# Last attention: query-key scores as two products of rounded parts, output copies on ScalarE, weight slabs dealt anew

## The reference

```
def stick_breaking_attention(q, k, v):
    ...
        valid = (key_pos[None, :] < q_pos[:, None]) & (key_pos[None, :] >= pad)
        zlog = jnp.einsum('bqhd,bkhd->bhqk', qi, kp) * scale
        log_beta = jax.nn.log_sigmoid(zlog)
        log_keep = jnp.where(valid, log_beta - zlog, 0.0)
        after = lax.cumsum(log_keep, axis=3, reverse=True) - log_keep
        w = jnp.where(valid, jnp.exp(log_beta + after), 0.0)
        return jnp.einsum('bhqk,bkhd->bqhd', w, vp)
```

## Time and profile before

| | us |
|---|---|
| median of 3 runs | 1615.33 (1614.38 to 1616.31) |
| the profiled execution: its own time | 1612.91 |
| its span in the trace | 1611.1 |
| busy in the span: TensorE (PE) | 1546.4 (96%) |
| VectorE (DVE) | 1024.8 (64%) |
| GpSimd (POOL) | 885.3 (55%) |
| ScalarE (ACT) | 507.3 (31%) |
| granted TensorE clock over the span | 0.992 |
| the last attention | about 850 to 1136 |

### The profile page before, as it was taken

How to read it: one execution, slowest core, us unless ns; L and a number is a source line. 1 busy time by engine, 2 the same in 40 slices (tenths; PEclk the granted TensorE clock), 3 DMA queues, 4 the chain that set the end, 5 groups by cost and what they waited for, 6 DMA issues and landing times.

```text
span 1611.1 us, 28791 instructions
## 1 busy us (share of the span) xinstructions
PE 1546.4 (96%) x10686; PEld 1352.3 (84%) x10686; DVE 1024.8 (64%) x1602; ACT 507.3 (31%) x1047; POOL 885.3 (55%) x830
## 2 busy tenths in 40 slices
PE   5999999999999999999988999998999999999998
PEld 4888877897888888999987888887998998988886
DVE  4499847469828876865767878875336666565002
ACT  4311012131137763333345555554214110111001
POOL 1455431567684408663428744344572777777981
PEclk9999999999999999999999999999999999999999
DMA  9437421323210002232111111112131333333331
GB/s 320 125 118 210 156 72 53 92 66 92 79 52 2 23 6 79 79 92 65 41 40 50 43 53 53 39 44 62 53 92 40 91 91 91 91 94 111 121 118 52
DMA packets 188971, 131.11 MB, mean 81 GB/s; under 512 B 5279, under 2 KB 171711, under 8 KB 188751
## 3 DMA queue, kind: packets, MB, share of 16 engines
q1 hardware_dynamic: 188878, 129.82, 26.5%
HBM read 127.71 MB, written 2.10 MB: 81 GB/s over the span
## 4 chain that ended last, share of the span: by engine, by line
PE 87%; DVE 7%; ACT 3%; issue 2%; DMA 1%; SPq 0%; DVEq 0%; ACTq 0%
PE ps L2316 20%; PE ps L2317 19%; PE ps L2319 19%; PE ps L3048 3%; PE ps L3047 3%; PE ps L3046 3%; PE ps L2640 2%; PE ps L2664 2%; PE ps L2961 2%; DVE sb_sum L2147 2%; PE ps L2627 1%; DMA ada_first<-in_ada_w 1%; DVE op_lo L1538 1%; PE ps L2869 1%; PE ps L2937 1%
## 5 line engine op out<-in xcount | busy, mean ns | idle before, releaser
L773 POOL TENSOR_SCALAR w_hi<-raw 128x512 fp32r<-128x512 f32 x322 | 244.4, 759 | 600.3 <-PE ps L2319 229.2
L775 POOL TENSOR_TENSOR w_lo<-raw,w_hi 128x512 fp32r<-128x512 f32 x322 | 462.2, 1435 | 26.8
L2316 PE MATMUL ps<-xn_hi,w_hi 128*128 128x264 f32 (+1 forms) x800 | 234.2, 313 | 8.5 <-ACT q_even L1285 3.3
L2316 PE MATMUL ps<-op_hi,w_hi 128*128 128x512 f32 x608 | 215.6, 355 | 1.6 <-DVE op_lo L1538 1.4
L2317 PE MATMUL ps<-xn_lo,w_hi 128*128 128x264 f32 (+1 forms) x800 | 212.7, 286 | 0.0
L2317 PE MATMUL ps<-op_lo,w_hi 128*128 128x512 f32 x608 | 204.9, 354 | 0.0
L2319 PE MATMUL ps<-op_hi,w_lo 128*128 128x512 f32 x608 | 177.9, 352 | 0.0
L2316 PEld LDWEIGHTS ps<-xn_hi,w_hi 128*128 128x128 f32 x800 | 152.1, 190 | 21.9 <-issue 13.5
L2316 PE MATMUL ps<-u_hi,w_hi 128*128 128x258 f32 (+1 forms) x528 | 162.1, 321 | 0.9 <-DVE u_lo L2208 0.4
L2319 PE MATMUL ps<-xn_hi,w_lo 128*128 128x264 f32 (+1 forms) x800 | 162.9, 285 | 0.0
L2317 PE MATMUL ps<-u_lo,w_hi 128*128 128x258 f32 (+1 forms) x528 | 162.0, 320 | 0.0
(11 more groups left out here) (458 smaller groups left out, 3211.2 us busy)
## 6 DMA issues: line engine op xcount, KB each, us to landing
raw<-in_w_in SPq DMA_DIRECT2D x45, 512.0 KB, 3.6
raw<-in_w_up SPq DMA_DIRECT2D x44, 512.0 KB, 3.7
ada_ring<-in_ada_w SPq DMA_DIRECT2D x14, 1024.0 KB, 5.3
raw<-in_w_down SPq DMA_DIRECT2D x22, 512.0 KB, 3.2
raw<-in_w_in_ab SPq DMA_DIRECT2D x20, 512.0 KB, 5.5
raw<-in_w_in_c SPq DMA_DIRECT2D x20, 512.0 KB, 3.7
ada_first<-in_ada_w SPq DMA_DIRECT2D x4, 2048.0 KB, 16.4
raw<-in_w_out SPq DMA_DIRECT2D x16, 512.0 KB, 3.8
```

The source lines that it names most:

```text
L773: steps(nc.gpsimd.tensor_scalar(hi, r, 1.0, 0.0, ALU.mult, ALU.add))
L775: nc.gpsimd.tensor_tensor(lo, r, hi.bitcast(F32), ALU.subtract)\
L2316: mm(o[:, 512 * b:512 * b + n], w_h[:, k, :], hi[:, k0 + k, c0:c0 + n], start=a, stop=False)
```

## The change

- **Scores.** Queries and keys are split into a rounded part and the rest, as the weights are. For each head of a pair, `qs` holds the rounded queries in the head's own 64 rows and their rest in the other 64 rows; `k1` holds the rounded keys in both halves; `k2` holds the rest of the keys in the head's own rows and zeros in the others. A score is then two fp32r products over 128 rows, q by `k1` and q by `k2`, in place of one fp32 product. Only unit 0 keeps plain fp32, with two products as well.
- **Copies of a slab.** `take` now copies the slab once to a staging tile `staged_sb`. `take_hi` makes the rounded parts of the two heads (two copies of 64 rows). `other_rows`, for keys only, copies the staged keys rounded into the other half (two more). GpSimd makes the rests in `low_parts`: two operations of 64 rows for queries and two for keys. `take` of keys waits for the rests of the queries, `take` of values for those of the keys (`sb_lo`); scores of a pair wait for `sb_hi` and `sb_lo`.
- **Output copies** go from VectorE to ScalarE, behind the copies of transposed weights of the step.
- **VectorE's step** begins with the scan; the operand for the norm comes last. The scan writes over its input (`sb_sum` is `sb_relu`), so that `sb_start` waits for an older transpose.
- **Tables.** `SB_CHUNKS` and `SB_TAKE` deal the chunks to other steps: queries are finished in step 3 (before: 4), keys in step 6 (7), values in step 0 (9 or 0). GpSimd's sum of squares moves one slab on.

```diff
-        SB_CHUNKS = {0: 4, 2: 3, 3: 3, 4: 2, 5: 3, 6: 3, 7: 2, 8: 4, 9: 4,
-                     11: 3, 12: 3, 13: 2, 14: 3, 15: 3, 16: 2, 17: 4}
-
-        SB_TAKE = {0: (0, 2, -1), 4: (1, 0, 0), 7: (1, 1, 1), 9: (1, 2, 2), 13: (0, 0, 3), 16: (0, 1, 4)}
+        SB_CHUNKS = {0: 3, 2: 4, 3: 4, 4: 3, 5: 2, 6: 3, 7: 2, 8: 3, 9: 3,
+                     11: 4, 12: 4, 13: 3, 14: 2, 15: 3, 16: 2, 17: 3}
+
+        SB_TAKE = {0: (0, 2, -1), 3: (1, 0, 0), 6: (1, 1, 1), 9: (1, 2, 2), 12: (0, 0, 3), 15: (0, 1, 4)}
...
+            def low_parts(pair, kind, splits):
+
+                m = pair % 2
+                pool.wait_ge(s["split"], splits)
+                pool.wait_ge(s["sb_hi"], 3 * pair + kind + 1)
+                for half in range(2):
+                    h = head_rows(half)
+                    if kind == 0:
+                        staged(nc.gpsimd.tensor_tensor(qs[m][head_rows(1 - half), half, :], staged_sb[h, :],
+                                                       qs[m][h, half, :].bitcast(F32), ALU.subtract))
+                    else:
+                        staged(nc.gpsimd.tensor_tensor(k2[m][half][h, :], staged_sb[h, :],
+                                                       k1[m][h, half, :].bitcast(F32), ALU.subtract))
+                pool.sem_inc(s["sb_lo"], 1)
...
             for g in range(-2, 24):
+                if g % 3 == 0:
+                    low_parts(g // 3, 1, g0 + 3 + g)
...
                 slab((g0 + 3 + g) // 2, (g0 + 3 + g) % 2, True)
+                if g % 3 == 2 and (g + 1) // 3 < SB_PAIRS:
+                    low_parts((g + 1) // 3, 0, g0 + 4 + g)
...
-                if g >= 4 and g % 3 == 1:
+                if g >= 5 and g % 3 == 2:
                     ysb_square(g // 3 - 1)
...
+            def take(m, kind, n, i=0):
+
+                act.wait_ge(s["slab_done"], g0 + n + 6 * i)
+                if kind:
+
+                    act.wait_ge(s["sb_lo"], (n - 1) // 3 * 2 + kind + 4 * i)
+                nc.scalar.activation(two(staged_sb[:, :]), seg2(gemm_ps[0]), ACT.Copy,
+                                     scale=1.0 if kind else ATT_SCALE).then_inc(s["sb_evac"], 1)
+
+            def take_hi(m, kind, n, i=0):
+
+                act.wait_ge(s["sb_evac"], n + 6 * i)
+                for half in range(2):
+                    h = head_rows(half)
+                    ins = nc.scalar.copy((k1 if kind else qs)[m][h, half, :], staged_sb[h, :])
+                ins.then_inc(s["sb_hi"], 1)
+
+            def other_rows(m):
+
+                for half in range(2):
+                    ins = nc.scalar.copy(k1[m][head_rows(1 - half), half, :], staged_sb[head_rows(half), :])
+                ins.then_inc(s["sb_hi"], 1)
...
+                    for w in sb_out_now(u - SB_SKEW) if sb_live(i, u - SB_SKEW) else ():
...
+                        act.wait_ge(s["sb_o"], 2 * NT * i + h + 1)
+                        o = sb_bank(w)[:, 0:n].unsqueeze(1)
+                        nc.scalar.copy(ysb[:, bass.ds(2 * i + m, 1), q0:q0 + n], o).then_inc(s["sb_y"], 1)
...
                     if u in SB_TAKE and (u <= len(SBU) or not last):
                         m, kind, g = SB_TAKE[u]
-                        take(m, kind, g0 + 3 + g + 1 + 6 * i)
+                        take(m, kind, 3 + g + 1, i)
+                        if kind == 1:
+                            take_hi(m, kind, 3 + g + 1, i)
                     if sb_scored(u + 1, last):
                         sb_logs(i, u + 1)
+                    if u in SB_TAKE and (u <= len(SBU) or not last):
+                        m, kind, g = SB_TAKE[u]
+                        if kind == 0:
+                            take_hi(m, kind, 3 + g + 1, i)
+                        if kind == 1:
+                            other_rows(m)
...
+                def scored(o, q_u, head, c0, c1, dt=F32R):
+
+                    mm(o, q_u.bitcast(dt), k1[m % 2][:, head, c0:c1].bitcast(dt), start=True, stop=False)
+                    return mm(o, q_u.bitcast(dt), k2[m % 2][head][:, c0:c1].bitcast(dt), start=False, stop=True)
```

More of the change, by code:

```diff
@@ L1277, in _ @@
             g0 = SLAB0["sb"]
[L1279 to L1283, removed]
-                        h = slice(HEAD * half, HEAD * half + HEAD)
-                        ins = nc.scalar.activation(two(qs[m][h, half, :]), seg2(gemm_ps[0][h, :]), ACT.Copy,
-                                                   scale=ATT_SCALE)
-                else:
-                    ins = nc.scalar.copy(two((ks, vs)[kind - 1][:, m, :]), seg2(gemm_ps[0]))
-                ins.then_inc(s["sb_evac"], 1)
+            def take(m, kind, n, i=0):
[14 more added lines that the diff above has]
+                ins.then_inc(s["sb_hi"], 1)
             def clear_other(m):
                 for half in range(2):
-                    h = slice(HEAD * (1 - half), HEAD * (2 - half))
-                    nc.scalar.copy(qs[m][h, half, :], zeros[h, 0:1].to_broadcast([HEAD, T2]))
+                    h = head_rows(1 - half)
+                    nc.scalar.copy(k2[m][half][h, :], zeros[h, 0:1].to_broadcast([HEAD, T2]))
             def chunk_in(i, j):
@@ L1319, in chunk @@
                         clear_other(0)
-                        take(0, 0, g0 + 1)
+                        take(0, 0, 1)
+                        take_hi(0, 0, 1)
                 if more:
@@ L1323, in chunk @@
                 else:
-                    take(0, 1, g0 + 2)
+                    take(0, 1, 2)
+                    take_hi(0, 1, 2)
+                    other_rows(0)
                 act.wait_ge(s["dec_in"], j + 1 + 2 * i)
@@ L2106, in sb_start @@
                 dve.wait_ge(s["sb_scores"], SBN * i + u + 1)
+                sb_wait(dve, "sb_wt", SBN, i, u - SB_BUFS + 1)
                 steps(nc.vector.tensor_tensor(own, own, mask[0:nq, :], ALU.add))
@@ L2162, in sb_iteration @@
                         sb_start(i, u + 1)
+                    if u - 1 in sb_norm(i):
+                        j = sb_norm(i)[u - 1]
+                        if not isinstance(i, int) or j:
+                            dve.wait_ge(s["op_hi"], OP_DONE["pre"] + sb_norm_chunk(i, j) + 1)
+                        else:
+                            dve.wait_ge(s["op_hi"], OP_DONE["pre"] + 1)
+                            dve.wait_ge(s["gated"], KC)
+                        nc.vector.scalar_tensor_tensor(ys_lo[:, bass.ds(sb_norm_chunk(i, j), 1), :],
+                                                       zs[:, bass.ds(sb_norm_chunk(i, j), 1), PAD:TP],
+                                                       cols[:, 0, bass.ds(sb_norm_chunk(i, j) + COL["ssd_norm"], 1)],
+                                                       ys_hi[:, bass.ds(sb_norm_chunk(i, j), 1), :].bitcast(F32),
+                                                       ALU.mult, ALU.subtract)\
+                          .then_inc(s["op_ready"], 1)
             steps(nc.vector.memset(v_sb[:, :, 0, :], 0.0))
@@ L2863, in sb_scores @@
                     for half in range(2):
-                        ins = mm(z_ps[32 * half:32 * half + 32, 0:META], qs[m % 2][:, half, 0:32],
-                                 ks[:, m % 2, 0:META], start=True, stop=True)
+                        ins = scored(z_ps[32 * half:32 * half + 32, 0:META], qs[m % 2][:, half, 0:32], half, 0, META, F32)
                 else:
@@ L2901, in sb_iteration @@
                 first = isinstance(i, int) and i == 0
-                chunk = 0 if first else -4
+                chunk = 0 if first else -3
                 for u in range(sb_steps(last)):
```

58 lines of the change are left out of this document (23 added, 35 removed).

## The result

The changed kernel took **1639.92 us** (median of 4, 1639.31 to 1641.24) against 1615.82 for the kernel before beside it (1614.38 to 1616.44): ratio **1.0153** (95% interval 1.0139 to 1.0167), slower by 24 us. Forecast was slower, by 6. The profiled run took 1639.48 us with a span of 1637.7 (before 1611.1).

A forecast was written before the change was run, and what follows sets the result against it. TensorE was taken as the bound, idling about 2 us per pair. Terms of +0.9 us a pair made +6.3 over seven pairs; with -3, +1 and +1.5 that is +5.8, so 1621 us, range 1602 to 1631.

The forecast's parts named there:

- ScalarE's queue, +3.1 us a pair: Key step: ScalarE takes 4.9 us up to unit 4's output copy; unit 8's scores wait, TensorE stands 3.1 us a pair.
- The second wait, +1.1: Behind unit 8's scores: the next exp takes 4.7 us to come, TensorE has 3.6 us of work, +1.1 us a pair.
- VectorE freed, -1.1: Output copies leave VectorE, so the scan runs earlier and TensorE waits less for unit 8's exp: -1.1 us a pair.
- The scores, -1.8 us a pair: Two rounded products replace one fp32 score product, saving 0.21, 0.31 and 0.38 us by width; two heads, -1.8 us a pair.
- Of both I take 4.0: TensorE's two waits, +3.1 for unit 4's output copy and +1.1 for the exp, counted together as +4.0 us a pair.
- The key copy, -0.4: TensorE's wait for the key slab copy before its next chunk gets output products of 0.81 us beside it: -0.4 us a pair.
- GpSimd, +0.2 a pair: Four more GpSimd operations per pair can stretch VectorE's scan, mostly where VectorE has slack: +0.2 us a pair, bounds 0 and +2.6.
- The last pair, -3: The last pair has no key step: -1.8 us from scores, and its 1.33 us wait for an exp goes, -3 us.
- The start, +1: Copies for pair 0 hold ScalarE until 841.2, past the SSD's `dec` at 840.29 on the chain: +1 us.
- the first pair, +1.5: GpSimd, nearly full in the first pairs, gets 5.2 us more; the key copy waits for the queries' rests: +1.5 us (0 to 5).

The follow-up runs named there:

- The key step's edits: Three edits of ScalarE's key step in the changed kernel: output copy ahead of logs, 1626.57 us; other head's rows behind next exp, 1628.16; all sorted by who waits, 1619.50.
- the filled run: Changed kernel with 8 fp32 matmuls of zeros on TensorE just ahead of unit 8's (17's) scores, inside the wait for ScalarE's output copy: 1635.24 us.
- the rests cut: Changed kernel with GpSimd's rests of queries and keys computed for 16 columns instead of 528 from pair 2 on: 1637.90 us.

## Why the prediction was right about the sign and wrong about the size

- **ScalarE's queue, +3.1 us a pair: right.** TensorE waited 3.1 us a turn (2.8 to 3.9, a turn's waits taken together), the queue took 5.2 us against 4.9, from the row of half copies at 1.28 for two. The key step's edits took back 13.3, 11.8 and 20.4 us of 24.
- **The second wait, +1.1, and VectorE freed, -1.1.** In sum right: listed waits for the exp are 1.5 us a turn before and after (2.1 with the clock full). The 2.6 us a pair from which the second was taken had counted stretches twice, since TensorE's weight load waits with its matmuls (6.6 of its 9.0 us lie inside their 11.6); the matmuls waited 1.5. In the run made for VectorE's part (the kernel before with ScalarE's output copies) the exp's waits did fall, by 0.8 us a turn, and the copies' waits took more than that.
- **The scores, -1.8 us a pair: the blocks were priced rightly, what stands around them was not.** From the start of a block to the second row behind it, in turns at full clock: 272 keys 0.58 to 0.37 us, 400 keys 0.79 to 0.49, 528 keys 1.20 to 0.81, which is the forecast's 0.21, 0.31 and 0.38. But the second block of 144 keys, put at nothing, got longer (0.36 to 0.59), and so did the meta block (0.40 to 0.47) and blocks right behind a wait (0.92 in place of 0.81), so that scores and the chunk product behind them give back 1.3 us a turn by their starts (11.8 to 10.5). And TensorE stops more often. At a stop, 0.29 us pass from the start of the last chunk product (L2366) to the end of its row, which no idle mark holds, where 0.12 to the next start is usual; there are five such stops in the third turn, one in the same turn before, and these products take 6.8 to 6.9 us to their successors' starts, from 6.1 (L2319). In all, a turn less its listed waits and the zeros is 30.8 us in the filled run (one drop left), from 31.8 before: -1.0.
- **The clock: no term at all.** With 3 us of standing still in each turn, it fell to 0.50 in four of six. In the changed kernel a turn less its listed waits is 32.0 us, so matmuls at half clock add 1.2 a turn; part of that hides waits (with the wait filled, those for the exp are 0.6 longer), and the net price is 0.5 a turn (4.7 us in the whole kernel). The prediction counted a waiting TensorE as idle time and nothing more. The steps that failed are this one ("Of both I take 4.0" priced a wait by its length alone) and the one on the scores, -1.8 for what is -1.0 at full clock.
- **The key copy, -0.4: nothing.** TensorE waited 0.5 us for its slab copies in five turns of six (1.3 in the first), from 0.4 before.
- **GpSimd, +0.2 a pair: right** (2.0 us in six pairs). The Trainium skill's rule of shared interfaces (GPSIMD Engine Reference, Specifications) holds in the rows: scans of 400 keys took 0.98 us with GpSimd idle and up to 1.81 beside it, and all 72 scans 74.1 us, 10% more than with the rests cut. But they had taken 77.3 in the kernel before, and little of it was on the path. What the prediction missed is GpSimd's backlog: 29.6 and 29.9 us busy in the first two turns. It became visible only when the queue was sorted.
- **The last pair, -3: less than half of it.** From unit 9's first scores to the last square of `ysb` (rows after, then before):

```profile
1110.39 0.25 PE L2912 MATMUL ps<-k_odd,q_odd 128*32 128x16 f32 x4
```

```profile
1163.01 0.65 ACT L1470 ACTIVATE sq<-ysb 128x528 f32<-128x528 f32 x1
```

```profile
1080.15 0.24 PE L2864 MATMUL ps<-ks,q_odd 128*32 128x16 f32 x4
```

```profile
1135.47 0.65 ACT L1414 ACTIVATE sq<-ysb 128x528 f32<-128x528 f32 x1 [3.50 <-DVE ysb L2138]
```

  From start to start 52.6 us against 55.3, -2.7; but at that point the new dealing has already done two chunks more (three since the key copy against one, 0.74 us each), so -1.2.
- **The start, +1, and the first pair, +1.5: right in size.** The first key copy came 0.7 us later and the second 1.1, though it stands 1.9 us of TensorE's work earlier in the new order (transposes 0.44, output products 0.81, unit 8's scores 0.65): +3.0 in all, against 2.5 and the first turn's 0.9.

Together: +1.1 to the second key copy, six turns +20.9, from the last key copy to the last square 62.4 us against 57.0, +5.5 (a key step's wait and drop, and the place of the copy), and -0.9 behind: the 26.6 us of span. Per turn, 3.5 measured against 0.9 forecast: the listed waits grew by 3.3 (the forecast's terms for waits make 4.0 - 1.1 - 0.4 + 0.2 = 2.7), and the time outside them by 0.2 (forecast -1.8), which is -1.0 of work and +1.2 of half clock. That the direction came out as forecast is no luck: the term that was to decide it, the queue, is there at its size. With the wait filled and the clock full in five of six turns, the turn is still 3.0 us longer.

## What to carry to other kernels

A wait of some 3 us on TensorE has a second price behind it, the clock (here 0.5 us a turn), so a change that saves matmul columns and pays with a wait can lose more than the wait. Sort an engine's queue by who waits for each entry before judging a move onto it: the same work in another order was worth 20 us here. And a saving on the engine that is the bound only counts where its feeders keep pace; the waits of before (1.9 us a turn) were a sign that they might not.

## What was not expected of the hardware

The granted clock fell to 0.50 (1.2 GHz) for 3.4 or 6.8 us in most, not all, turns with a wait of 2.8 to 3.8 us, and the kernel got 4.7 us faster by 1.95 us of zero products in the wait. In the third and fifth turns the same wait (3.02 and 3.03 us) left the clock at 1.00; what decides between the two was not found. Nor does it take 3 us: with the other head's rows moved, the clock fell behind a wait of 1.69 us (at 1030.3), and with the old dealing behind one of 1.97 (at 995.6). The Trainium skill (TensorE: Matmul & The Clock Gate, What's actually happening) says that the clock has two levels and follows how busy TensorE was of late; the rows agree in both, 1.00 and 0.50.
